# One chunk's taps in another bank, and two steps of VectorE in another order, in a fused two-block transformer kernel

## What is computed

```python
def conformer_conv(x, w_in, b_in, conv_w, conv_b, ln_g, ln_b, w_out, b_out):
    a, g = jnp.split(x @ w_in + b_in, 2, axis=-1)
    h = a * jax.nn.sigmoid(g)
    h = lax.conv_general_dilated(
        h, conv_w[:, None, :].astype(h.dtype), window_strides=(1,),
        padding=[(CONV_KERNEL - 1, 0)], dimension_numbers=("NWC", "WIO", "NWC"),
        feature_group_count=D_MODEL) + conv_b
    h = jax.nn.silu(layer_norm(h, ln_g, ln_b))
    return h @ w_out + b_out
```

## Time and profile before

| | us |
|---|---|
| median of 3 runs | 1448.79 |
| lowest and highest | 1448.34, 1451.68 |
| profiled execution | 1449.69 |
| span in its profile | 1447.9 |
| PE busy | 1429.1 |
| DVE busy | 918.1 |
| ACT busy | 614.2 |
| POOL busy | 226.6 |

### The profile page before, as it was taken

The page is one execution under the profiler, slowest core; times in us unless marked ns, Lnnn a source line. Parts: engine busy times, 40 slices in busy tenths (PEclk is TensorE's granted clock), DMA queues, the critical chain, the costliest instruction groups (busy, mean ns, idle before and its releaser), DMA issues.

```text
span 1447.9 us, 19992 instructions
## 1 busy us (share of the span) xinstructions
PE 1429.1 (99%) x6886; PEld 1168.4 (81%) x6886; DVE 918.1 (63%) x1320; ACT 614.2 (42%) x914; POOL 226.6 (16%) x172
## 2 busy tenths in 40 slices
PE   8999999999999999999999999899999999999999
PEld 7788888888887898888888888666588888888887
DVE  7877773573655667767754756889888653544532
ACT  5544442342546665444432424668554322222210
POOL 7100000000302231000000004599711000000000
PEclk9999999999999999999999999999999999999999
DMA  5233233232431012332332332249713332332321
GB/s 191 88 101 102 88 101 116 73 101 91 122 102 59 30 60 88 101 102 87 102 116 73 101 98 91 88 112 227 194 53 102 116 103 88 100 102 88 101 95 51
DMA packets 49756, 144.95 MB, mean 100 GB/s; under 512 B 10016, under 2 KB 10784, under 8 KB 49696
## 3 DMA queue, kind: packets, MB, share of 16 engines
q1 hardware_dynamic: 47408, 137.34, 30.0%
q0 software_dynamic: 1440, 5.24, 2.0%
q10 hardware_dynamic: 848, 1.59, 0.3%
HBM read 135.14 MB, written 2.10 MB: 95 GB/s over the span
## 4 chain that ended last, share of the span: by engine, by line
PE 91%; POOL 4%; issue 2%; DMA 1%; DVE 1%; ACT 1%; SPq 0%; ACTq 0%; POOLq 0%; DVEq 0%
PE bank L628 29%; PE bank L630 28%; PE bank L629 28%; POOL prod L614 2%; PE bank L779 1%; PE bank L807 1%; POOL res L563 1%; PE bank L792 1%; DMA shifted<-hc 1%; DMA res<-xT 1%; POOL ssum L573 1%; PE bank L906 1%; PE bank L966 0%; PE bank L965 0%; PE bank L672 0%
## 5 line engine op out<-in xcount | busy, mean ns | idle before, releaser
L628 PE MATMUL bank<-xh,whi 128*128 128x512 f32 x1184 | 465.4, 393 | 0.2
L630 PE MATMUL bank<-xh,wlo 128*128 128x512 f32 x1184 | 461.4, 390 | 0.0
L629 PE MATMUL bank<-xl,whi 128*128 128x512 f32 x1184 | 461.3, 390 | 0.0
L988 ACT ACTIVATE whi<-raw 128x1024 fp32r<-128x1024 f32 x244 | 255.6, 1050 | 242.0 <-PE bank L630 237.7
L1349 DVE TENSOR_TENSOR wlo<-raw,whi 128x1024 fp32r<-128x1024 f32 x230 | 287.9, 1252 | 42.8 <-ACT whi L988 34.7
L628 PEld LDWEIGHTS bank<-xh,whi 128*128 128x128 f32 x1184 | 222.4, 188 | 53.7 <-issue 5.2
L630 PEld LDWEIGHTS bank<-xh,wlo 128*128 128x128 f32 x1184 | 222.4, 188 | 46.6
L629 PEld LDWEIGHTS bank<-xl,whi 128*128 128x128 f32 x1184 | 222.5, 188 | 46.1 <-issue 1.0
L630 PE MATMUL bank<-ahi,wlo 128*128 128x512 f32 x608 | 236.8, 389 | 0.0
L628 PE MATMUL bank<-ahi,whi 128*128 128x512 f32 x608 | 236.8, 389 | 0.0
L629 PE MATMUL bank<-alo,whi 128*128 128x512 f32 x608 | 236.8, 389 | 0.0
(11 more groups left out here) (191 smaller groups left out, 1312.0 us busy)
## 6 DMA issues: line engine op xcount, KB each, us to landing
raw<-w_ffn_up SPq DMA_DIRECT2D x88, 512.0 KB, 3.4
raw<-w_ffn_down SPq DMA_DIRECT2D x32, 512.0 KB, 3.3
raw<-w_mlp_up SPq DMA_DIRECT2D x32, 512.0 KB, 3.3
raw<-w_mlp_down SPq DMA_DIRECT2D x32, 512.0 KB, 3.3
raw<-w_ain SPq DMA_DIRECT2D x16, 512.0 KB, 3.6
raw<-w_ffn_down SPq DMA_DIRECT2D x16, 384.0 KB, 3.0
raw<-w_qkv SPq DMA_DIRECT2D x12, 512.0 KB, 3.5
raw<-w_wo SPq DMA_DIRECT2D x8, 512.0 KB, 3.3
```

Of the source, the lines that this page charges most:

```text
L628: nc.tensor.matmul(out_, hi, mh, start=first, stop=False)
L629: nc.tensor.matmul(out_, hi, ml, start=False, stop=False)
L630: return nc.tensor.matmul(out_, lo, mh, start=False, stop=last)
L988: nc.scalar.activation(whi[:, s, 0:tiles * P], raw[:, s, 0:tiles * P], ACT.Copy)\
```

## The change

Chunk 0 becomes a second chunk whose own taps are kept apart: in bank 5, the last one written to `hv`. Its convolution matmuls start bank 6 afresh and do not wait for the taps; its collect takes the extra addition that chunk 7 has. The eviction of chunk 1's value to bank 5 waits for those taps. The matmul that wrote to bank 6 ahead of the stage is dropped. And on VectorE `gated(c + 1)` moves from the start of iteration c + 1 to the end of iteration c, ahead of `collect(c - 1)`, as it stood for chunk 7 already; `diagonals(7)` moves into iteration 6, before its round 5. Line numbers after the change differ from those before by up to 2.

```diff
-APART = C - 1
+APART = (0, C - 1)
...
+LAST_DIAGONALS = 5
...
                     if name == "ain" and t == 0:
-                        for b in range(2):
-                            nc.tensor.matmul(bank[6 + b][:], whi[:, 0, 0:P], xh[:, 0, :], start=True, stop=True)
+                        nc.tensor.matmul(bank[7][:], whi[:, 0, 0:P], xh[:, 0, :], start=True, stop=True)
...
-                if c != APART:
+                if c not in APART:
                     pe.wait_ge(tap_steps, sum(len(own_taps(e)) for e in range(c + 1)))
...
-                                              start=(q == 0 and c == APART), stop=(q == ROUNDS[c] - 1),
+                                              start=(q == 0 and c in APART), stop=(q == ROUNDS[c] - 1),
...
-                at = taps[:] if c == APART else bank[6 + c % 2][:]
+                at = taps[:] if c in APART else bank[6 + c % 2][:]
                 if n == 0:
-                    if 2 <= c != APART:
+                    if c >= 2 and c not in APART:
                         dve.wait_ge(hv_ready, c - 1)
...
-                V.scalar_tensor_tensor(hv[:, c, :] if c == APART and n == len(own_taps(c)) - 1 else at, x, w, at,
+                V.scalar_tensor_tensor(hv[:, c, :] if c in APART and n == len(own_taps(c)) - 1 else at, x, w, at,
...
-                if c == APART:
+                if c in APART:
                     dve.wait_ge(tap_steps, sum(len(own_taps(j)) for j in range(c + 1)))
                     V.tensor_tensor(hv[:, c, :], part, hv[:, c, :], ALU.add).then_inc(own_added, 1)
                     part = hv[:, c, :]
-                    dve.wait_ge(own_added, 1)
+                    dve.wait_ge(own_added, APART.index(c) + 1)
...
                 dve.wait_ge(chain_done, p.chain + 2 * c + j + 1)
+                if j and c - 1 in APART:
+                    dve.wait_ge(tap_steps, sum(len(own_taps(e)) for e in range(c)))
...
-                if c < C - 1:
-                    gated(c)
+                    gated(0)
                 if c < C - 1:
                     diagonals(c)
...
+                    if n == LAST_DIAGONALS and c == C - 2:
+                        diagonals(C - 1)
...
-                if c == C - 2:
-                    diagonals(C - 1)
-                    gated(C - 1)
+                if c < C - 1:
+                    gated(c + 1)
                 if c:
                     collect(c - 1)
```

## The result

Median of five executions: 1454.98 us after (1451.0 to 1455.94), 1449.17 us before (1448.34 to 1451.68). The ratio is 1.003, with a 95% interval of 1.0019 to 1.0042. So the change makes the kernel slower, by 3 to 6 us, and the 1450.4 of the prediction, with its upper end of 1452.2, was too low.

A forecast was written before the change was run, and what follows sets the result against it. The prediction took TensorE as the bound, busy 1429.1 of 1447.9 us. It summed -0.2 (matmul), +0.5 (new add) and +1.35 (clock) to +1.65 us, forecasting 1450.4 from the median of 1448.79, range 1447.0 to 1452.2.

The forecast's parts named there:

- The dropped matmul: Warm-up matmul (L656) ahead of the stage's first chain: removing it moves everything, the pivot too, by -0.2 us.
- The pivot: Wait of 2.06 us before chunk 3's convolution, set by GpSimd through ScalarE's gate: TensorE's earlier gains are waited away there.
- The order part: VectorE's gate c+1 ahead of collecting c-1: chunk 2's hc some 1.9 us earlier, but no later step gains, so 0.
- GpSimd without waits, its end near 1039.4: Expected sign in the new profile: GpSimd still runs without waits and ends its adds within 1 us of 1039.4.
- GpSimd shows waits: One of the prediction's conditions for being wrong: any waits of GpSimd in the new profile.
- The new add: Collecting chunk 0: VectorE's extra addition slows GpSimd over shared SBUF access, +0.5 us, ends 0 and 0.9.
- The 0.7 us before conv 1: TensorE waits 0.7 us for chunk 1's own taps before its convolution, leaving a lead of 3.2 us.
- Absorbed by the later wait: A clock fall in the 3.5 us gap before unit 5 would cost nothing, absorbed by the wait before chunk 3.
- The term of the clock, +1.35: Behind a 5.3 us wait before chunk 3's convolution, TensorE's clock falls: +1.35 us, ends 0 and 1.4.
- Nothing later absorbs it: After chunk 3's convolution, near 986, the summed loss of +1.65 us stays in full to the end.
- I am wrong if TensorE waits for anything between 987 and 1027: One of the prediction's conditions for being wrong: any TensorE wait between 987 and 1027 us, after chunk 3's convolution begins.
- Rival 4: Last copies of chunks 3 to 6 land later among weight loads, 1.5 us each: +6, 1455 us; chance 0.05.

The follow-up runs named there:

- experiment 6: Changed kernel, with ScalarE's sigmoid of the next chunk's gate issued one to three products earlier in chunks 1 to 4; 1450.45 us, ratio 1.0004.
- experiment 3: Kernel before, with only VectorE's new order and chunk 0's taps still in bank 6; 1450.07 us, ratio 1.0004.
- experiment 2: Changed kernel with VectorE's old order, so only the bank apart and the dropped matmul; 1452.41 us, ratio 1.0021.
- experiment 1: Changed kernel run again without any edit, for a second trace and comparison; 1452.83 us, ratio 1.002.
- experiment 5: Kernel before, made late by 11 unused matmuls behind the first convolution matmuls of chunk 3 (2.72 us); 1453.65 us, ratio 1.0036.
- experiment 12: As experiment 4, with GpSimd's accumulating DMAs for the low parts of units 14 and 15 issued later; 1450.0 us, ratio 1.0.
- experiment 4: Changed kernel, with 22 unused matmuls keeping TensorE busy in the wait ahead of the convolution of chunk 3; 1451.17 us, ratio 1.0011.
- 9: As experiment 6, with two products of chunk 7 moved from GpSimd to VectorE and its last low parts two steps earlier; 1447.81 us, ratio 0.9987.
- 11: As 9, with 13 unused matmuls ahead of unit 5 to keep TensorE busy there; 1446.69 us, ratio 0.9978.
- experiment 7: Kernel before, with the same earlier sigmoid as experiment 6; 1449.6 us, ratio 0.9997.
- 10: As experiment 7, with the product and low-part edits of 9, without bank apart or new order; 1450.38 us, ratio 1.0004.

## Why the prediction failed

**Right.** The wait for the taps vanished and conv 0 starts at once (6.32 instead of 12.33). The wait of L629 for VectorE's L1349 is 3.43 us, predicted 3.5. The dropped matmul is worth what was said: from L656 to the first `hc` it is 17.75 us before and 17.52 after. The pivot held: conv 3 stands at 57.04 against 56.89, whatever TensorE did ahead of it, and experiment 6 shows that it is the gate behind GpSimd's sums. The order part is worth 0 in this kernel (experiment 3). TensorE is at 0.50 behind 986.

**GpSimd without waits, its end near 1039.4**: the number came out (1039.39), the reason did not. GpSimd's timeline of after has a wait that before does not have:

```profile
1032.42 1.28 POOL L615 TENSOR_TENSOR prod<-tapped 128x512 f32<-128x512 f32 x1 [2.10 <-ACT tapped L1261]
```

The products of the last chunk come from the last `hc`, which TensorE now made 3.1 us late, so that GpSimd's slack of some microsecond ran out there. Counted from the first `hc`, its last sum ends at 112.1 (before 110.4); only the early start of this execution hid that. So even "GpSimd shows waits" among the conditions for being wrong came true. It is a consequence of the two losses, not a third one.

**The new add**: +0.5 predicted, ends 0 and 0.9. VectorE's timeline of after has it at 955.63, and GpSimd's has its two adds beside it:

```profile
955.63 0.69 DVE L1739 TENSOR_TENSOR hv<-prod,hv 128x512 f32<-128x512 f32 x1
```

```profile
954.43 3.04 POOL L615 TENSOR_TENSOR prod<-prod,tapped 128x512 f32<-128x512 f32 x2
```

Two adds at the mean of the earlier trace rows take 2.78, so some 0.3 us is lost; `hc` of chunk 3 comes at 44.06 instead of 43.68, 0.38 later. It comes with the bank and not with the order: experiment 2, with the new add, has 44.02, experiment 3, without it, 43.67. The step was sound and a little dear. By the Trainium skill ("SBUF — State Buffer", section "SBUF: two separate sides") whichever of the two engines starts first has the shared ports for its whole instruction; if that were VectorE all through, GpSimd would lose the whole 0.69 us of the add, and the trace has about half of it.

**The 0.7 us before conv 1**: absent. The clock fell already behind the 3.43 us at unit 5, as the text held possible, and the slower matmuls brought TensorE to conv 1 at 26.64 (25.48 in experiment 1) where the prediction has 24.3. So the lead was 0.9 to 2.0 us and not 3.2, and the wait at chunk 3 was 3.09 and 4.25 us and not 5.3. "Absorbed by the later wait" was right.

**The term of the clock, +1.35**: mechanism right, size too small. It cost 1.62, 2.74 and 1.3 us in the three traces with the bank apart and nothing done against it (after, experiments 1 and 2). The prediction took it from one execution, in which the low stretch was 3.4 us long. Around chunks 0, 1 and 3 it is either 3.4 or 6.8 us in the traces, and the kernel of before has the long one too (experiment 5, where conv 0 took 5.39 us, 2.6 more than at full clock). With the wait shorter than predicted the clock was still lost: 3.09 us of idle was enough. A price from a single occurrence needed an upper end of about twice itself; with ends of "0 and 1.4" the range could not hold what came.

**"Nothing later absorbs it"**: this step failed, in the direction that it did not look. Nothing absorbed the lateness, but something added to it. At conv 4 TensorE was 1.8 us late, at the last `hc` 3.1 (2.9 and 4.5 in experiment 1), since TensorE's lateness moves the copies of chunk 5, while GpSimd's accumulating DMAs stay at their time, and the copies fell among them. This is the sentence "I am wrong if TensorE waits for anything between 987 and 1027", and it did, at 1014.89.

**Rival 4** had this place in part (last copies landing later under a moved transfer, chunks 3 to 6) and got 0.05. It named the wrong agent: the weight loads stand behind the copies on SP's queue in every run, in experiment 12 as well, where the wait is gone; GpSimd's DMAs are the agent. And its wait came at one chunk, not at four. What would have raised its chance was in the trace: the copies of chunk 5 landed 0.2 us before TensorE's convolution started. The prediction gives the landings of chunks 0 and 3, and nowhere sets those of the other chunks, where TensorE just did not wait, against the time at which it came.

**The sum as it was**: -0.2 for the dropped matmul, +0.15 from the first `hc` to conv 3 (the forecast had +0.5 there), +1.6 for the clock, +1.3 for the copies; +2.9 us in this trace, +4.2 in the second, where the forecast had +1.65. **Open** is the rest of the first comparison, 5.8 us in the median against 2.9 in its trace; the second comparison gave 3.4, against 4.2 in its trace, whose first `hc` also came early. Four of the first five executions took over 1454 us, and none of these was profiled; the long form of the clock's fall (2.7 us) together with the wait for copies would give most of it, and a fall at the end of the stage (0.8 us or more, experiment 4) could give more, but that is only argued.

## What to carry to other kernels

A wait removed ahead of a fixed point is moved, not saved; before costing it at nothing, ask what the moved wait does to the clock, and give a clock price read from one row a wide upper end. Then follow the lateness further: list every transfer on the way that lands with less than a microsecond to spare, and what else is issued at a time that doesn't move with it. And find the next two limits (here the gate, then GpSimd's last sum): only with both out of the way did the change pay (experiments 9 and 11). When a limit is moved and the time stays, look at the granted clock behind it too: in experiment 7 a gain of 1.15 us had arrived and was lost to a fall of the clock right behind.

## What the runs showed of the hardware

- At unit 5 and chunk 3 the clock fell with idle stretches of 3.09, 3.43 and 4.25 us, and not with one of 2.06 us. It fell inside the wait (944.6 in after, 983.6 in experiment 1) or up to 1.2 us after the matmuls had resumed (chunk 3 of after). At the end of the stage, where waits and short groups of matmuls alternate, it fell in some traces with no wait above 1.00 us (experiments 4, 7, 10 and 11). So the length of one wait does not tell it.
- How long it stayed at 0.50 differs between executions of one kernel: after has 6.8 us at unit 5 and 3.4 at chunk 3, experiment 1 the reverse; at the end of the stage in experiment 6 it was 10.2 us.
- Two DMAs that accumulate into SBUF, issued among four copies and not behind them, made the last copy land 5 us later (8.7 us after the first issue in experiment 12, 13.7 in experiment 4). In experiments 6 and 9 the copies of chunk 5 were all issued ahead of these DMAs, and the slowest took 5.4 and 6.1 us to land.
- A float32 matmul of 128x128 by 128 columns shows as two records of about 0.115 us each (22 matmuls, 44 records, 5.07 us).
- The first 20 us of the program, the same code in both kernels, differ by execution. TensorE's share there, first in before, then in after:

```profile
0.00:20.00 20.00, 16.21 (x75) 13.98 (x76) 13.46 (x56) 11.38 (x20) 11.12 (x18) 1.00 0.80 287
```

```profile
0.00:20.00 20.00, 18.15 (x78) 15.98 (x79) 13.82 (x58) 11.99 (x21) 12.22 (x18) 1.00 0.80 291
```

TensorE was busy 1.9 us longer in after's, and this is the start by which its stage lay ahead (L656 at 909.77 against 911.36). A comparison of two spans would have hidden more than half of what the stage lost.
